# Two hybrid transformer blocks on one core: weight units laid out as contiguous blocks, and x loaded first in the weights' queue

## What is computed

```
cond = jax.nn.silu(c)
for l in range(DEPTH):
    mod = cond @ w_ada[l] + b_ada[l]
    sh1, sc1, g1, sh2, sc2, g2 = [m[:, None, :] for m in jnp.split(mod, 6, axis=-1)]
    h = _layer_norm(x) * (1.0 + sc1) + sh1
    mix = _mixer(h, w_in[l], ...)
    x = _layer_norm(DN_ALPHA * x + g1 * mix, ln1_g[l], ln1_b[l])
    h = _layer_norm(x) * (1.0 + sc2) + sh2
    ffn = _moe(h, w_router, router_bias, w_exp_gate[l], w_exp_up[l], w_exp_down[l])
    x = _layer_norm(DN_ALPHA * x + g2 * ffn, ln2_g[l], ln2_b[l])
```

## Time and profile before

| | |
|---|---|
| median of 3 runs | 1745.12 us (1743.94 to 1749.65) |
| profiled execution, its own time | 1743.22 us |
| its span, first to last instruction | 1741.4 us |
| TensorE busy | 1671.8 us (96%) |
| VectorE, ScalarE, GpSimd busy | 1210.3, 932.9, 241.0 us |
| mean granted TensorE clock | 0.981 of full |
| read from memory | 390.46 MB, 225 GB/s over the span |

### The profile page before, as it was taken

One profiled execution on the slowest core, in us unless ns is written; L12 is line 12 of the kernel. 1 busy time (PEld: TensorE's weight loads), 2 busy tenths in 40 slices (PEclk: granted clock), 3 DMA queues, 4 the chain that ended last, 5 costly groups with the idle time before them and its releaser, 6 DMA issues.

```text
span 1741.4 us, 24621 instructions
## 1 busy us (share of the span) xinstructions
PE 1671.8 (96%) x10100; PEld 1413.2 (81%) x10100; DVE 1210.3 (70%) x1372; ACT 932.9 (54%) x1052; POOL 241.0 (14%) x216
## 2 busy tenths in 40 slices
PE   4999998999899998999989999999999999999999
PEld 2887876888689896788867899878888899978887
DVE  2547668899975857989986585566667655657664
ACT  4435545877544644688756463554436655445342
POOL 0420020000034001001016402000001710210000
PEclk8999998999999998999999999999999999999999
DMA  9975586999855245799938345556655634536552
GB/s 381 331 278 194 215 313 251 379 375 377 308 178 170 98 146 222 291 384 374 339 110 278 124 143 170 178 171 209 216 169 195 204 123 144 191 123 218 193 193 73
DMA packets 172479, 393.11 MB, mean 226 GB/s; under 512 B 6128, under 2 KB 110576, under 8 KB 150352
## 3 DMA queue, kind: packets, MB, share of 16 engines
q1 hardware_dynamic: 169952, 381.71, 61.9%
q0 software_dynamic: 1712, 7.50, 1.2%
q10 hardware_dynamic: 704, 2.33, 0.3%
HBM read 390.46 MB, written 1.05 MB: 225 GB/s over the span
## 4 chain that ended last, share of the span: by engine, by line
PE 76%; DVE 7%; POOL 6%; issue 5%; ACT 4%; DMA 1%; POOLq 0%; ACTq 0%; DVEq 0%
PE ps L585 18%; PE ps L587 18%; PE ps L586 18%; PE ps L645 6%; PE ps L646 3%; DVE low L2014 2%; PE ps L718 2%; ACT whi L1409 2%; POOL TB L2959 1%; PE ps L920 1%; PE ps L888 1%; PE ps L903 1%; PE ps L649 1%; DMA xs<-in_x 1%; PE ps L603 1%
## 5 line engine op out<-in xcount | busy, mean ns | idle before, releaser
L2014 DVE TENSOR_TENSOR low<-raw,whi 128x2048 fp32r<-128x2048 f32 x310 | 711.0, 2303 | 288.0 <-ACT whi L1409 286.3
L1409 ACT ACTIVATE whi<-raw 128x2048 fp32r<-128x2048 f32 x310 | 590.7, 1913 | 284.4 <-PE ps L587 215.9
L585 PE MATMUL ps<-HH,whi 128*128 128x256 f32 x960 | 275.6, 287 | 0.0
L586 PE MATMUL ps<-HH,whi 128*128 128x256 f32 x960 | 271.5, 283 | 0.0
L587 PE MATMUL ps<-HH,low 128*128 128x256 f32 x960 | 271.5, 283 | 0.0
L585 PE MATMUL ps<-whi,HH 128*128 128x512 f32 (+1 forms) x640 | 247.6, 387 | 17.4 <-DVE low L2014 7.2
L587 PE MATMUL ps<-whi,HH 128*128 128x512 f32 (+1 forms) x640 | 243.1, 380 | 0.0
L586 PE MATMUL ps<-low,HH 128*128 128x512 f32 (+1 forms) x640 | 243.1, 380 | 0.0
L585 PEld LDWEIGHTS ps<-HH,whi 128*128 128x128 f32 x960 | 183.9, 192 | 13.6 <-issue 13.2
L586 PEld LDWEIGHTS ps<-HH,whi 128*128 128x128 f32 x960 | 184.0, 192 | 0.0
L587 PEld LDWEIGHTS ps<-HH,low 128*128 128x128 f32 x960 | 183.9, 192 | 0.0
(11 more groups left out here) (351 smaller groups left out, 2530.2 us busy)
## 6 DMA issues: line engine op xcount, KB each, us to landing
raw<-in_w_gu SPq DMA_DIRECT2D x80, 1024.0 KB, 5.2
raw<-in_w_ff SPq DMA_DIRECT2D x66, 1024.0 KB, 5.0
raw<-in_w_in SPq DMA_DIRECT2D x58, 1024.0 KB, 5.4
raw<-in_w_d SPq DMA_DIRECT2D x40, 1024.0 KB, 5.4
raw<-in_w_gate SPq DMA_DIRECT2D x32, 1024.0 KB, 5.4
ada<-in_w_ada_s SPq DMA_DIRECT2D x16, 1024.0 KB, 7.2
raw<-in_w_out SPq DMA_DIRECT2D x16, 1024.0 KB, 5.1
AR<-in_w_ada_s SPq DMA_DIRECT2D x13, 1024.0 KB, 8.8
```

Source lines behind the costliest of these rows:

```text
L585: pe.matmul(out, lhs[0], rhs[0], start=start, stop=False)
L586: pe.matmul(out, lhs[0], rhs[1], start=False, stop=False)
L1409: act.activation(wide(i, whi), wide(i, raw), ACT.Copy).then_inc(*up("w_hi", i))
L2014: dve.tensor_tensor(wide(i, low), wide(i, raw), wide(i, whi).bitcast(F32), ALU.subtract).then_inc(*up("w_lo", i))
```

## The change

The host now lays out every static unit as the block of 128 rows of 8 KB that the expert units already are, and stacks the 190 blocks into one tensor `w_u`. The bytes of a unit, and where each lands in `raw`, stay as they were. The load of x leaves ScalarE's queue and becomes SP's first DMA, ahead of modulation step 0. In ScalarE's queue `cols` now goes ahead of `cons`.

```diff
+def by_partition(w, k):
+    return w.reshape(k, P, -1).transpose(1, 0, 2).reshape(P, -1)
+
 def unit8(w, c0):
-    return w[:, c0:c0 + S].rearrange("(k p) c -> p k c", p=P), 8, S
+    return by_partition(w[:, c0:c0 + S], 8), 8, S

 def unit4(w, a, c0):
-    return w[a * 512:(a + 1) * 512, c0:c0 + 512].rearrange("(k p) c -> p k c", p=P), 4, 512
+    return by_partition(w[a * 512:(a + 1) * 512, c0:c0 + 512], 4), 4, 512

 def unit2(w):
-    return w.rearrange("(k p) c -> p k c", p=P), 2, D
+    return by_partition(w, 2), 2, D
...
             def fetch(i):
-                out, name = blocked(i, raw), order[i]
-                if units[name][0] is not None:
-                    sp.dma_start(out, units[name][0]).then_inc(*up(f"raw{i % NRAW}", i, by=16))
+                name = order[i]
+                if name in laid_out:
+                    sp.dma_start(wide(i, raw), dr["w_u"][laid_out[name]]).then_inc(*up(f"raw{i % NRAW}", i, by=16))
...
+            sp.dma_start(x[:, :, :], dr["x"].rearrange("(t p) d -> p t d", p=P)).then_inc(*up("x_in", by=16))
             for s in range(8):
                 load_mod(sp, s)
             load(4)
...
+            act.dma_start(cols[:, :], dr["cols"]).then_inc(*up("cols_in", by=16))
             act.dma_start(cons[:, :], dr["cons"]).then_inc(*up("cons_in", by=16))
-            act.dma_start(cols[:, :], dr["cols"]).then_inc(*up("cols_in", by=16))
-            act.dma_start(x[:, :, :], dr["x"].rearrange("(t p) d -> p t d", p=P)).then_inc(*up("x_in", by=16))
             act.wait_ge(*at("cons_in"))
...
+    units = weight_units({...})
     arrays = {
-        "x": a["x"][0], "mem": a["mem_2"][0], "cols": cols, "rows": rows, "na_b": na,
...
+        "x": a["x"][0], "w_u": np.stack([w for w, _, _ in units.values() if w is not None]), "mem": a["mem_2"][0], "cols": cols, "rows": rows, "na_b": na,
```

More of the change, by code:

```diff
@@ L163, with weight_units @@
 BRANCH_ORDER = (1, 0, 2, 3)
-def weight_units(dr):
+def weight_units(ws):
     out = {}
     for l in range(L):
-        w = dr["w_in"][l]
+        w = ws["w_in"][l]
         for a in range(2):
@@ L180, in weight_units @@
             out["A", l, "gate", i] = unit8(w, 3072 + S * i)
-        out["A", l, "pb"] = unit2(dr["w_pb"][l])
+        out["A", l, "pb"] = unit2(ws["w_pb"][l])
         for a in range(2):
-            out["A", l, "pa", a] = dr["w_pa"][l][:, a * 512:a * 512 + 512].rearrange("(k p) c -> p k c", p=P), 4, 512
+            out["A", l, "pa", a] = by_partition(ws["w_pa"][l][:, a * 512:a * 512 + 512], 4), 4, 512
         for i in range(4):
-            out["A", l, "out", i] = unit4(dr["w_out"][l], i % 2, 512 * (i // 2))
+            out["A", l, "out", i] = unit4(ws["w_out"][l], i % 2, 512 * (i // 2))
         for name in MOE_ORDER:
@@ L188, in weight_units @@
     for l in range(L):
-        w = dr["w_in2"][l]
-        for n, m, i in (("mkv", dr["w_kv"][l], 0), ("rqk", w, 0), ("rvg", w, 2), ("nqk", w, 5), ("pv", w, 4), ("nvmq", w, 7)):
+        w = ws["w_in2"][l]
+        for n, m, i in (("mkv", ws["w_kv"][l], 0), ("rqk", w, 0), ("rvg", w, 2), ("nqk", w, 5), ("pv", w, 4), ("nvmq", w, 7)):
             if n == "pv":
@@ L197, in weight_units @@
             for i in range(4):
-                out["B", l, "gate", n, i] = unit8(dr["w_gate"][l], n * D + S * i)
+                out["B", l, "gate", n, i] = unit8(ws["w_gate"][l], n * D + S * i)
         for z, n in enumerate(BRANCH_ORDER):
@@ L201, in weight_units @@
                 for i in range(4):
-                    out["B", l, "gate", n, i] = unit8(dr["w_gate"][l], n * D + S * i)
-            out["B", l, "br", n] = unit2(dr["w_br"][l, n])
+                    out["B", l, "gate", n, i] = unit8(ws["w_gate"][l], n * D + S * i)
+            out["B", l, "br", n] = unit2(ws["w_br"][l, n])
             if z == 0:
                 for i in range(4):
-                    out["B", l, "gate", 2, i] = unit8(dr["w_gate"][l], 2 * D + S * i)
+                    out["B", l, "gate", 2, i] = unit8(ws["w_gate"][l], 2 * D + S * i)
         for i in range(4):
-            out["B", l, "out", i] = unit4(dr["w_out2"][l], i % 2, 512 * (i // 2))
-        wf, wd = dr["w_ff1"][l], dr["w_ff2"][l]
+            out["B", l, "out", i] = unit4(ws["w_out2"][l], i % 2, 512 * (i // 2))
+        wf, wd = ws["w_ff1"][l], ws["w_ff2"][l]
         for i in range(2):
@@ L242, with build @@
 TURNS = [(p, g) for p in range(6) for g in range(PARTS[p])]
-def build(nc, dr):
+def build(nc, dr, units):
     ctx = ExitStack()
@@ L279, in build @@
         psum = [ctx.enter_context(nc.psum_tensor(f"ps{i}", [P, 512], F32)) for i in range(8)]
-        units = weight_units(dr)
         order = list(units)
+        laid_out = [name for name in order if units[name][0] is not None]
+        laid_out = {name: i for i, name in enumerate(laid_out)}
         number = {n: i for i, n in enumerate(order)}
@@ L3042 @@
     ada = np.stack([np.concatenate([ada[l, k, :, part, h] for (l, part, h), k in mod_chunks(s)], 1) for s in range(48)])
+    units = weight_units({
+        "w_in": a["w_in"], "w_pa": a["w_branch_a"], "w_pb": a["w_branch_b"], "w_out": a["w_out"], "w_in2": a["w_in_2"],
+        "w_gate": a["w_gate_2"], "w_kv": a["w_mem_kv_2"], "w_br": a["w_branch_2"], "w_out2": a["w_out_2"], "w_ff1": ff1, "w_ff2": a["w_ffn_out_2"]})
     arrays = {
-        "x": a["x"][0], "mem": a["mem_2"][0], "cols": cols, "rows": rows, "na_b": na,
-        "w_ada_s": ada, "w_in": a["w_in"], "w_pa": a["w_branch_a"], "w_pb": a["w_branch_b"],
-        "w_out": a["w_out"], "ln1_g": a["ln1_g"], "ln1_b": a["ln1_b"], "ln2_g": a["ln2_g"], "ln2_b": a["ln2_b"],
+        "x": a["x"][0], "w_u": np.stack([w for w, _, _ in units.values() if w is not None]), "mem": a["mem_2"][0], "cols": cols, "rows": rows, "na_b": na,
+        "w_ada_s": ada, "ln1_g": a["ln1_g"], "ln1_b": a["ln1_b"], "ln2_g": a["ln2_g"], "ln2_b": a["ln2_b"],
         "w_gu": first, "w_d": a["w_exp_down"].reshape(L, NE, 2, P, D).transpose(0, 1, 3, 2, 4).reshape(L, NE, P, 2 * D),
-        "w_in2": a["w_in_2"], "w_gate": a["w_gate_2"], "w_kv": a["w_mem_kv_2"], "w_br": a["w_branch_2"],
-        "w_out2": a["w_out_2"], "w_ff1": ff1, "w_ff2": a["w_ffn_out_2"],
     }
@@ L3059 @@
     dr["out"] = nc.dram_tensor("out_0", (S, D), F32, kind="ExternalOutput").ap()
-    build(nc, dr)
+    build(nc, dr, units)
     r = run_bass_kernel_spmd(nc, [feed], core_ids=[0])
```

## The result

The changed kernel takes 1741.16 us in the median of 22 runs (1736.64 to 1746.09), the kernel before 1744.74 us in the median of 22 (1739.70 to 1749.65). The ratio is 0.9982, 95% interval 0.9974 to 0.9991: about 3.1 us less, between 1.6 and 4.5. That is a gain clear of zero, and within the 0.3% that the forecast counted as "same".

A forecast was written before the change was run, and what follows sets the result against it. TensorE, busy 1671.8 of 1741.4 us, was taken as the bound, with the head set by the load of x. Layout nothing, early x 2.5 us: 1745.1 - 2.5 = 1742.6 us, range 1737 to 1747.

The forecast's parts named there:

- The likeliest case: Whole run: the head gives 2.5 us (1.3 to 3.4) and the rest nothing, 1742.6 us; chance 0.5.
- The layout costs and gives nothing: Static unit loads: larger pieces save transfer time, but the six-deep ring hides it after the head; costed at nothing.
- x sets the head: Head: x, loaded first, lands at about 7.5 us, 10 us sooner; first product starts 2.6 to 3.4 us sooner.
- Step 3 and then step 7 set it next: Head: TensorE waits for modulation step 3 until 17.74 us, then step 7, starting at 27.5 us instead of 30.85.
- rival 2: Head: low TensorE clock when modulation step 7 lands leaves a gain of 1.0 us or less, about 1744.1; chance 0.18.
- The first layer norm: ScalarE in the head: starts at 8 us and ends near 13, instead of ending at 22.7; sign: done by 14.
- The rule of the Trainium skill: TensorE's clock: the low rate is the default and activity releases it; no size given.
- The deduction for the clock: First products: if the clock recovers at the same moment, half the 2.6 to 3.4 us is lost; 2.5 taken.
- SP issues units 0 to 3 in about 2 us: SP's queue in the head: fewer pieces mean hardly any stall, against 23.95 us before; costed at nothing.
- Unit 4 is next and costs nothing: After the head: unit 4, late behind modulation steps 8 to 11, is covered by four units' products; costed at nothing.
- Rival 3: End of first expert stage: waits of 1.8 us (AR) and 2.3 (ada) also vanish, 1738.5 or 1736 us; chance 0.24.
- Rival 4: Gaps between stages: one more low-clock stretch costs 6.9 us, giving 1749.5 us; chance 0.08.

The follow-up runs named there:

- x first alone: Against the kernel before: x first in SP's queue and cols ahead of cons, with the old layout of smaller rows; ratio 0.9984 (0.9973 to 0.9995).
- the layout alone: Against the kernel before: only the static units' layout changed, x still third in ScalarE's queue; ratio 1.0008 (0.9998 to 1.0019).
- x behind step 3: Against the changed kernel: x loaded behind modulation steps 0 to 3 in SP's queue; ratio to the kernel before 1.0010 (0.9998 to 1.0022).
- second look: The changed kernel profiled once more with nothing changed; first product at 35.10 us, modulation step 8 at 59.19 us; no ratio given.
- warm head: Changed kernel plus unread matmuls: eight before the first product, twelve at the start, two behind each of modulation steps 0 to 2; ratio to before 1.0001.
- x behind step 1: Against the changed kernel: x loaded behind modulation steps 0 and 1 in SP's queue; ratio to the kernel before 0.9990 (0.9980 to 0.9999).
- cons first: Against the changed kernel: cons loaded ahead of cols again, as before the change; first product at 35.51 us, no ratio given.

## Why the prediction was right, and where it was not

The forecast was 2.5 us (1742.6 on the scale of the median then known); measured are 3.1, between 1.6 and 4.5. The likeliest case was the right one, by its own mechanism.

- *The layout costs and gives nothing.* Shown within the intervals, of about 0.1% to either side: x first alone has the whole gain, and the layout alone has none. In the head's saturated queue unit 0 came some 0.2 us sooner with it (its cast starts at 29.65 us, and at 29.89 with x first alone, where it waited for the unit). The cast was not what the product waited for last.
- *x sets the head.* Shown by the kernel with x behind step 3, which has all of the change but the early x and is back at 38.59 us.
- *Step 3 and then step 7 set it next.* Right as to the loads. The copy of group 0 was forecast for 18.8 us and started at 19.25, because step 3 took 1.94 us and not 1.06. Step 7 was forecast to start at 27.5: its load was there by 27.2, but TensorE, still at its low clock behind the transposes, started it at 27.94. That is rival 2 in small. The first product was forecast for 35.3 to 36.1 and started at 35.77. That this lies inside is in part luck: with TensorE in time it starts at 35.10, 35.04 and 34.95 us (second look, x first alone twice), a little ahead of the forecast.
- *The first layer norm* was to start at 8 us and be done by 14. It started at 9.25 and ended at 14.45: `cons` landed at 9.1 us, and `cpad`, which ScalarE computes first, came at 9.14 and not at 8. Nothing hung on it, since the copy stood at 19.25.
- *The rule of the Trainium skill* that was put beside the clock (TensorE: Matmul & The Clock Gate, Part 1: The HAM clock gate), by which activity releases the clock, agrees with the warm head: step 0 takes 1.06 us behind the added matmuls, and 1.94 us in the changed kernel, where TensorE had done nothing before. The profile's granted clock reads 1.00 in both.
- *The deduction for the clock* was the term that was mis-sized. I took 2.5 for fear that the low clock would end at the same moment as before and take half of what was won. It did not: it fell and rose 2.5 us earlier as well (0.52 from 34.3 to 41.1 us, before from 36.8 to 43.6). The head's 2.9 us arrived at step 8 as 2.7. In the second look the low stretch ended at about 38.1 us, with only seven slow products and not twelve, and the head's 3.6 us arrived as 4.3. The difference between 2.5 and the measured 3.1 is smaller than the interval, so the time by itself does not show this.
- *SP issues units 0 to 3 in about 2 us*: it took 7.08. The queue still fills. Nothing hung on it.
- *Unit 4 is next and costs nothing*: right, and closer than thought. Its cast waited 7.3 us for it, at 52.48 us, and TensorE went on with what it had.
- *Rival 3* (waits for modulation steps behind static units near 470 us) is out: the longest waits for AR and `ada` are still 1.8 and 1.9 us. *Rival 4* (more low clock) happened in the one profile, 0.978 against 0.981. Over the 22 runs of the changed kernel the median of the mean clock is 0.981. But the low stretch between 460 and 500 us, which cost this profile 2.2 us, is in every profile but the one before the change, so a small part of this rival stays open.

What stays open: whether the layout has a small cost later in the run. Its own ratio is 1.0008 (0.9998 to 1.0019), that of x behind step 3, which has it too, is 1.0010 (0.9998 to 1.0022), and in four of the eleven profiles with it a modulation step issued near 211 us landed 1.3 to 3 us late. Against it: with x early the ratios with and without it are 0.9982 and 0.9984.

## What to carry to other kernels

When a load at the head of a kernel is late, ask for the landing that its consumer really needs, and put it in the queue just ahead of that; sooner gives nothing, as x behind two steps showed. Before changing the layout of transfers, look whether anyone waits for them: a saving of up to 0.5 us a unit over 190 units was hidden by a ring of six buffers, and even in a saturated stage 0.4 us a unit came out as a sixth of the sum. A gain of 3 us in 1740 is seen in the head of the trace and in many medians, not in the spans of two profiles.

## What the runs showed of the hardware

- One program gets its low-clock stretches at different times in different executions. The changed kernel was granted 0.89 between 425 and 440 us in one profile and 1.00 in the other, and its low stretch around the first products lay from 34.3 to 41.1 us in one (0.52) and from 31.4 to 38.1 us in the other (0.50).
- The profile's granted clock can read 1.00 where TensorE is slow. In the first 16 us it is 1.00 in every profile, and step 0 takes 1.94 us where the same eight matmuls take 1.06 in the warm head. In the second look it is 1.00 up to 31 us, and the transposes at 21.7 us still take 1.95 us where they take 1.07 at 30 us. The durations of equal instructions decide.
- A load shares the engines with what the other queue moves beside it. `cons`, first in its queue both times, landed in 6.2 us beside modulation steps (8 KB rows, before the change) and in 4.2 us beside x (4 KB rows, cons first); `cols`, first in its queue both times, in 5.9 us beside modulation steps (x behind step 1) and in 4.1 us beside x (changed kernel).
- Small rows cost engine time: the engines were no less busy and moved 364 GB/s with 1 KB, 389 with 2 KB and 422 with 8 KB rows, and 185 against 262 GB/s between 2 and 4 us with rows of 512 bytes among them (busy for 0.75 and 0.81).
- Matmuls whose result nobody reads are not free even in a gap. At the low clock eight of them took 5.1 us.
